# Attention scores and values as full 128-row products, lower parts of the keys kept beside zeros

## The reference, cut to what matters

```python
# first block: 8 heads, strictly causal ("mixer")
z = einsum('bhqd,bhkd->bhqk', q_blk, k_c) * scale       # 128 queries, keys 0..end
sp = where(valid, softplus(z), 0.0)
rem = cumsum(sp, axis=3, reverse=True) - sp
a = where(valid, exp(log_sigmoid(z) - rem), 0.0)
outs.append(einsum('bhqk,bhkd->bhqd', a, v_c))

# second block: 16 heads ("fox")
s = einsum('bhqd,bhkd->bhqk', q[:, :, lo:hi], k[:, :, :hi]) * scale
s = s + cum[:, :, lo:hi, None] - cum[:, :, None, :hi]
s = where(kpos[None, :] <= qpos[:, None], s, -1e30)
outs.append(einsum('bhqk,bhkd->bhqd', softmax(s), v[:, :, :hi]))
```

## Time and profile before

| | before |
|---|---|
| median of three runs | 2120.28 us |
| time of the profiled execution | 2121.13 us |
| its span in the trace | 2119.9 us |
| PE busy | 2077.3 us (98%) |
| DVE busy | 1101.9 us (52%) |
| ACT busy | 836.4 us (39%) |
| POOL busy | 289.0 us (14%) |
| share of PE in the chain that ended last | 92% |
| granted TensorE clock, mean | 0.992 |

### The profile page before, as it was taken

The page is one execution under the profiler, slowest core; times in us unless marked ns, Lnnn a source line. Parts: engine busy times, 40 slices in busy tenths (PEclk is TensorE's granted clock), DMA queues, the critical chain, the costliest instruction groups (busy, mean ns, idle before and its releaser), DMA issues.

```text
span 2119.9 us, 24127 instructions
## 1 busy us (share of the span) xinstructions
PE 2077.3 (98%) x9440; PEld 1695.1 (80%) x9440; DVE 1101.9 (52%) x1570; ACT 836.4 (39%) x1200; POOL 289.0 (14%) x215
## 2 busy tenths in 40 slices
PE   5999999999999999999999999999999999999998
PEld 4788888788877878888888877777788888888888
DVE  8655655624554654333336444443456566464666
ACT  3322222435655533222224455554333343242343
POOL 3000000001101210000000343443000022021120
PEclk8999999999999999999999999999999999999999
DMA  7665554422223533333223332332433423232232
GB/s 289 230 198 189 190 188 131 165 101 80 70 75 100 175 109 110 100 98 92 98 76 121 127 106 100 100 105 100 173 115 129 144 91 99 99 91 98 87 98 85
DMA packets 84401, 261.31 MB, mean 123 GB/s; under 512 B 9264, under 2 KB 13488, under 8 KB 84288
## 3 DMA queue, kind: packets, MB, share of 16 engines
q1 hardware_dynamic: 84288, 259.77, 37.2%
HBM read 242.92 MB, written 16.81 MB: 123 GB/s over the span
## 4 chain that ended last, share of the span: by engine, by line
PE 92%; DVE 4%; ACT 2%; issue 1%; DMA 1%; POOL 0%; SPq 0%; DVEq 0%; ACTq 0%; POOLq 0%
PE P L729 28%; PE P L731 28%; PE P L730 28%; PE P L930 2%; DVE ADA L1925 1%; PE P L1108 1%; PE P L942 1%; PE P L941 1%; PE P L1099 0%; DMA WRAW<-w_in_zv 0%; PE P L944 0%; DVE SQ L1912 0%; PE P L834 0%; PE P L1155 0%; PE P L822 0%
## 5 line engine op out<-in xcount | busy, mean ns | idle before, releaser
L729 PE MATMUL P<-UH,WH 128*128 128x512 f32 (+1 forms) x1848 | 719.4, 389 | 12.2 <-POOL UL L2729 10.7
L731 PE MATMUL P<-UH,WL 128*128 128x512 f32 (+1 forms) x1848 | 714.3, 387 | 0.0
L730 PE MATMUL P<-UL,WH 128*128 128x512 f32 (+1 forms) x1848 | 713.7, 386 | 0.0
L584 ACT ACTIVATE WH<-WRAW 128x1024 fp32r<-128x1024 f32 (+1 forms) x345 | 359.0, 1043 | 840.0 <-PE P L731 827.4
L599 DVE TENSOR_TENSOR WL<-WRAW,WH 128x1024 fp32r<-128x1024 f32 (+1 forms) x286 | 355.1, 1245 | 206.5 <-ACT WH L584 205.8
L729 PEld LDWEIGHTS P<-UH,WH 128*128 128x128 f32 x1848 | 348.1, 188 | 86.7 <-POOL UL L2729 10.0
L731 PEld LDWEIGHTS P<-UH,WL 128*128 128x128 f32 x1848 | 347.8, 188 | 71.0
L730 PEld LDWEIGHTS P<-UL,WH 128*128 128x128 f32 x1848 | 348.1, 188 | 68.5
L729 PE MATMUL P<-AH,WH 128*128 128x512 f32 x544 | 215.6, 396 | 0.0
L731 PE MATMUL P<-AH,WL 128*128 128x512 f32 x544 | 215.2, 396 | 0.0
L730 PE MATMUL P<-AL,WH 128*128 128x512 f32 x544 | 215.1, 395 | 0.0
(11 more groups left out here) (285 smaller groups left out, 2234.2 us busy)
## 6 DMA issues: line engine op xcount, KB each, us to landing
WRAW<-w_gu SPq DMA_DIRECT2D x88, 512.0 KB, 3.5
ADA<-w_ada SPq DMA_DIRECT2D x72, 512.0 KB, 4.7
WRAW<-w_down SPq DMA_DIRECT2D x48, 512.0 KB, 3.6
WRAW<-w_up SPq DMA_DIRECT2D x44, 512.0 KB, 3.5
WRAW<-w_in SPq DMA_DIRECT2D x40, 512.0 KB, 3.5
WRAW<-w_mix SPq DMA_DIRECT2D x36, 512.0 KB, 3.4
WRAW<-w_down SPq DMA_DIRECT2D x24, 384.0 KB, 3.1
WRAW<-w_out SPq DMA_DIRECT2D x16, 512.0 KB, 4.0
```

The lines of the kernel that those rows point to most:

```text
L584: s.act.activation(hi, s.mem.WRAW[:, c % 4, :self.order[c][2]], FN.Copy).then_inc(*self.rounded.inc(c))
L729: pe.matmul(out, wh, xh, start=start, stop=False, skip_group_check=True)
L730: pe.matmul(out, wh, xl, start=False, stop=False, skip_group_check=True)
L731: return pe.matmul(out, wl, xh, start=False, stop=stop, skip_group_check=True)
```

## The change

The keys' lower part gets a tile for each head of a pair, `KL0` and `KL1`, of the same shape as `K`; the rows that the head does not own hold zeros, written once per attention by POOL (`pool_zeros`). The second product of each strip then reads 128 rows. The last block is treated as the other three: two split products of 128 columns in the scores, two in the values. `T3`, `V31`, `V32`, `P3` and the ACT copies that filled them go. In fox the transposed last block lies beside block 1 in PSUM bank 6, and one ACT copy and one DVE subtraction of 512 columns take both (they were 128 and 384 columns on ACT, 384 on DVE). The mask products and the mixer's unsplit running-sum products (lines 1007, 1009) stay as they are.

```diff
+TURNED = [(2, 4, 1024, 256), (1, 6, 512, 512), (0, 5, 0, 512)]
...
-        kl = put(e + "KL", [128, 2, S], F32R)
-        t3 = [put(e + n + "3", [128, 2, 128], F32) for n in ("Q", "K")]
+        kl = [put(e + "KL0", [128, 2, S], F32R), put(e + "KL1", [128, 2, S], F32R)]
...
-def pe_products(s, out, Q, K, KL, h, a, b, keys_first):
+def pe_products(s, out, Q, K, KL, h, a, b, keys_first, start=True):
     p, e = (h // 2) % 2, h % 2
-    rows = head_rows(h)[0]
-    for i, (q, k) in enumerate([(Q[e][:, p, a], K[e][:, p, b]),
-                                (Q[e][rows, p, a], KL[rows, p, b])]):
-        x, y = (k, q) if keys_first else (q, k)
-        s.pe.matmul(out, x, y, start=i == 0, stop=False, skip_group_check=True)
+    for i, k in enumerate((K[e], KL[e])):
+        x, y = Q[e][:, p, a], k[:, p, b]
+        if keys_first:
+            x, y = y, x
+        s.pe.matmul(out, x, y, start=start and i == 0, stop=False, skip_group_check=True)
...
-    for j in range(3):
+    for j in range(4):
         of = slice(OFF[j], OFF[j] + WID[j])
         v = V[:, j, 128 * h:128 * h + 128]
         pe.matmul(ob[:, 128 * j:S], v, hi[:, of], start=j == 0, stop=False, skip_group_check=True)
-        pe.matmul(ob[:, 128 * j:S], v, lo[:, of], start=False, stop=j == 2, skip_group_check=True)
-    rows = head_rows(h)[0]
-    pe.matmul(s.P[rows, 7, 384:S], V3[:, 64 * h:64 * h + 64], own, start=False, stop=True,
-              skip_group_check=True).then_inc(*s.value.inc(name, h))
+        last = pe.matmul(ob[:, 128 * j:S], v, lo[:, of], start=False, stop=j == 3,
+                         skip_group_check=True)
+    last.then_inc(*s.value.inc(name, h))
...
-        for j in range(3):
+        for j in range(4):
             pe_products(s, Z[:, OFF[j]:OFF[j] + WID[j]], mem.Qa, mem.Ka, mem.KLa, h,
-                        slice(128 * j, S), slice(j * 128, (j + 1) * 128), True)
-        pe.matmul(Z[:, OFF[3]:OFF[3] + 128], mem.T3a[1][rows, p, :], mem.T3a[0][rows, p, :],
-                  start=False, stop=False, skip_group_check=True)
+                        slice(128 * j, S), slice(j * 128, (j + 1) * 128), True, j < 3)
...
-            if i == 0:
-                pe.matmul(z, mem.T3b[0][rows, p, :], mem.T3b[1][rows, p, :], start=False,
-                          stop=False, skip_group_check=True)
-            else:
-                if i == 1 and h:
-                    on.wait_ge(*s.pt_lo(h - 1, 2))
-                pe_products(s, z, mem.Qb, mem.Kb, mem.KLb, h, slice(i * 128, (i + 1) * 128),
-                            slice(0, 128 * (i + 1)), False)
+            if i == 1 and h:
+                on.wait_ge(*s.pt_lo(h - 1, 2))
+            pe_products(s, z, mem.Qb, mem.Kb, mem.KLb, h, slice(i * 128, (i + 1) * 128),
+                        slice(0, 128 * (i + 1)), False, i > 0)
...
-        block(h, 3, 6, 384)
-        block(h, 1, 6, 0).then_inc(*s.turned.inc(h, 1))
+        block(h, 3, 6, 0)
+        block(h, 1, 6, 128).then_inc(*s.turned.inc(h, 1))
...
-    act.activation(T3[w][:, p % 2, :], src[:, own], FN.Copy, scale=scale)
...
 def dve_pairs(s, e, w, p, Q, K, KL, src, scale):
     s.on_dve.wait_ge(*s.qk_hi(e, w, p))
+    s.on_dve.wait_ge(*s.kl_zero(e))
...
-        lo = KL[rows, p % 2, :] if w else X[other, p % 2, :]
+        lo = KL[h][rows, p % 2, :] if w else X[other, p % 2, :]
...
+def pool_zeros(s, e, KL):
+    s.pool.memset(KL[0][:, :, :].bitcast(F32), 0.0)
+    s.pool.memset(KL[1][:, :, :].bitcast(F32), 0.0).then_inc(*s.kl_zero.inc(e))
...
     pool_norm(s, "ffn1", "start")
+    on.wait_ge(*s.ple_mm(3))
+    on.wait_ge(*s.u_lo("ffn1", KD - 1))
+    pool_zeros(s, "a", mem.KLa)
...
     pool_power(s, mem.R[:, 8:12], mem.VAR[:, 4:8], "ffn2", 1)
+    on.wait_ge(*W.done(W.at["ffn2", "down", 2, KD - 1]))
+    on.wait_ge(*s.x_row(KD - 1))
+    pool_zeros(s, "b", mem.KLb)
```

More of the change, by code:

```diff
@@ L284, in __init__ @@
         self.expo = new("expo", [(h, i) for h in range(16) for i in (3, 2, 1, 0)])
-        self.pt_hi = new("pt_hi", [(h, x) for h in range(16) for x in (2, 3, 1, 0)])
+        self.pt_hi = new("pt_hi", [(h, x) for h in range(16) for x in (2, 1, 0)])
         self.zv = new("zv", [(half, tb) for half in range(2) for tb in range(4)])
@@ L361, in __init__ @@
         self.merged = new("merged", [(m,) for m in tiles])
+        self.kl_zero = new("kl_zero", [("a",), ("b",)])
         self.prob = new("prob", [(h, i) for h in range(16) for i in (3, 2, 1, 0)])
@@ L451, in mix @@
         self.V1 = put("V1", [128, 4, 1024], F32R)
-        self.V31 = put("V31", [128, 512], F32)
         self.pairs("a")
@@ L463, in pairs @@
         k = [put(e + "K0", [128, 2, S], F32R), put(e + "K1", [128, 2, S], F32R)]
-        kl = put(e + "KL", [128, 2, S], F32R)
-        t3 = [put(e + n + "3", [128, 2, 128], F32) for n in ("Q", "K")]
+        kl = [put(e + "KL0", [128, 2, S], F32R), put(e + "KL1", [128, 2, S], F32R)]
         if e == "a":
-            self.Qa, self.Ka, self.KLa, self.T3a = q, k, kl, t3
+            self.Qa, self.Ka, self.KLa = q, k, kl
         else:
-            self.Qb, self.Kb, self.KLb, self.T3b = q, k, kl, t3
+            self.Qb, self.Kb, self.KLb = q, k, kl
     def second(self):
@@ L481, in fox @@
         self.V2 = put("V2", [128, 4, 2 * D], F32R)
-        self.V32 = put("V32", [128, D], F32)
         self.pairs("b")
-        self.P3 = put("P3", [128, 128], F32)
         self.T2 = put("T2", [128, 1280], F32)
@@ L919, in pe_first, with pe_values @@
     pe_norm(s, "ffn1", 0, s.mem.AH1, s.mem.AL1)
-def pe_products(s, out, Q, K, KL, h, a, b, keys_first):
+def pe_products(s, out, Q, K, KL, h, a, b, keys_first, start=True):
     p, e = (h // 2) % 2, h % 2
-    rows = head_rows(h)[0]
-    for i, (q, k) in enumerate([(Q[e][:, p, a], K[e][:, p, b]),
-                                (Q[e][rows, p, a], KL[rows, p, b])]):
-        x, y = (k, q) if keys_first else (q, k)
-        s.pe.matmul(out, x, y, start=i == 0, stop=False, skip_group_check=True)
-def pe_values(s, V, V3, name, h, hi, lo, own, free):
+    for i, k in enumerate((K[e], KL[e])):
[3 more added lines that the diff above has]
+        s.pe.matmul(out, x, y, start=start and i == 0, stop=False, skip_group_check=True)
+def pe_values(s, V, name, h, hi, lo, free):
     pe, ob = s.pe, s.P[:, 7, :]
@@ L976, in pe_mixer @@
     for h in range(8):
-        p, rows = (h // 2) % 2, head_rows(h)[0]
         on.wait_ge(*s.qk_lo("a", 0, h // 2))
@@ L1023, in pe_mixer @@
         free.append(s.o_sum("a", h - 1) if h else s.small)
-        pe_values(s, mem.V1, mem.V31, "a", h, mem.SH, mem.SL, own, free)
+        pe_values(s, mem.V1, "a", h, mem.SH, mem.SL, free)
     assert not fillers
@@ L1125, in values @@
         free.append(s.o_sum("b", h - 1) if h else s.small)
-        pe_values(s, mem.V2, mem.V32, "b", h, mem.PH, mem.PL, mem.P3[:, :], free)
+        pe_values(s, mem.V2, "b", h, mem.PH, mem.PL, free)
     fill()
@@ L1401, in act_first_square, with act_pairs @@
     act_square(s, "ffn1", m, s.mem.H[:, m, :], s.sums("start", 0))
-def act_pairs(s, e, w, p, Q, K, T3, src, own, scale, free):
+def act_pairs(s, e, w, p, Q, K, src, scale, free):
     act, on = s.act, s.on_act
@@ L1440, in v_evac @@
         on.wait_ge(*s.u_lo("ffn1", KD - 1))
[L1441 to L1444, removed]
+        act.activation(hi, by_head(src), FN.Copy).then_inc(*s.v_hi.inc("mix v", tb))
     def ga_evac(m):
@@ L1455, in qk_evac @@
         free = [W.done(W.at[tag]), s.score("a", 2 * p - 3) if p >= 2 else s.sums("ffn1", 0)]
-        act_pairs(s, "a", w, p, mem.Qa, mem.Ka, mem.T3a, s.psum(*tag), slice(384, 512),
-                  0.125 if w == 0 else 1.0, free)
+        act_pairs(s, "a", w, p, mem.Qa, mem.Ka, s.psum(*tag), 0.125 if w == 0 else 1.0, free)
     def evac(kind, m):
@@ L1630, in v_evac @@
         on.wait_ge(*W.done(W.at["ffn2", "down", 2, KD - 1]))
[L1631 to L1634, removed]
+        act.activation(hi, by_head(src), FN.Copy, scale=r).then_inc(
+            *s.v_hi.inc("fox v", half, tb))
     def qk_evac(w, p):
         free = [s.qk_raw(w, p), s.score("b", 2 * p - 3) if p >= 2 else s.sums("ffn2", 1)]
-        act_pairs(s, "b", w, p, mem.Qb, mem.Kb, mem.T3b, mem.TMP[:, w, :], slice(0, 128), 1.0,
-                  free)
+        act_pairs(s, "b", w, p, mem.Qb, mem.Kb, mem.TMP[:, w, :], 1.0, free)
     for q in range(4):
@@ L1689, in turned @@
     def turned(h):
-        def upper(j, bank, n):
+        for j, bank, at, n in TURNED:
             on.wait_ge(*s.turned(h, j))
@@ L1693, in upper @@
                 on.wait_ge(*s.value("b", h - 1))
-            act.activation(mem.PH[:, OFF[j]:OFF[j] + n], s.P[:, bank, 0:n], FN.Copy).then_inc(
+            act.activation(mem.PH[:, at:at + n], s.P[:, bank, 0:n], FN.Copy).then_inc(
                 *s.pt_hi.inc(h, j))
[L1697 to L1703, removed]
     fill(1)
@@ L2416, in turned @@
     def turned(h):
-        for j, bank, w in ((2, 4, 256), (1, 6, 384), (0, 5, 512)):
-            x = slice(OFF[j], OFF[j] + w)
+        for j, bank, at, w in TURNED:
```

(1 more changed line is left out.)

## The result

| | before | changed |
|---|---|---|
| median | 2120.36 us (4 runs, 2119.91 to 2120.60) | 2086.74 us (4 runs, 2085.97 to 2086.94) |
| profiled execution | 2121.13 us, span 2119.9 | 2086.63 us, span 2085.4 |

The ratio is 0.984, with a 95% interval from 0.9828 to 0.9853: 33.6 us faster. The forecast was 2101.7 us with a range from 2088.0 to 2111.0. The direction was right; the gain is 1.8 times the one forecast, and the time lies just under the range.

The account below looks back on a forecast made before the run. PE, busy 98% of the span, was taken as the bound. Savings of 7.2 + 10.7 + 2.1 + 0.2 = 20.2 us less 1.6 given back, net 18.6, took 2120.28 to 2101.7 us; range 2088 to 2111.

Parts of the forecast that it names:

- mixer scores: Mixer, first score product to masks: 2.45 us becomes 1.55, saving 0.90 per head, 7.2 us in 8 heads.
- mixer values and next scores: Mixer values, 1.50 us before, save 0.02 per head, 0.2 us in all; the scores that follow save 0.90.
- fox scores: Fox's score products with four masks: 2.95 us becomes 2.28, saving 0.67 per head, 10.7 us in 16 heads.
- fox values: Fox's value products: 1.61 us becomes 1.48, saving 0.13 per head, 2.1 us in 16 heads.
- given back in the mixer: Mixer savings lost to waits: 1.4 us in heads 1 and 3, 0.1 each in heads 6 and 7; 1.6 in all.
- x: Cost of a 128-column split product, two in each head's scores and two in its values, 96 in all; taken as 0.22 us.
- The rival with x = 0.11: Narrow split products in scores and values are cheap: 28.8 us saved, 2091.5 us; chance 0.33.
- s: Passage from a full-row product into a bf16 mask, one per mixer head, four per fox head, 72 in all; taken as 0.07 us.
- The rival's other end: Cheap narrow split products at x = 0.06: 33.6 us saved, 2086.7 us; the cheap-products case had chance 0.33.
- The mechanism: In score pairs, each passage from 128 to 64 rows or back costs about 0.19 us; the change takes it out.
- The give-back at `RL`: Mixer line 1015, PE waiting for DVE's RL: heads 1 and 3 gain 0.2, not 0.90, each; 1.4 us back.
- The rival with dear masks: Masks cost more than the rows did: s = 0.33 leaves no gain, s = 0.40 gives 2125.5 us; chance 0.03.

Follow-up runs that it names:

- The probe: Changed kernel with eight added matmuls of varied width, rows and type ahead of each fox head's values, to price them; 2112.85 us, run once, only its trace used.
- the second experiment: Changed kernel with the second product of each score pair read on the head's own 64 rows again; 2112.03 us, 25.3 slower.
- The run with both holds: Changed kernel with fox's masks last, three POOL subtractions in the mixer held until RL, and the next ones in heads 1 and 3 held too; 2081.66 us.

## Why the prediction was wrong

The table sets the forecast's savings per head beside what the timelines of both kernels show. A phase is read from its first product to the second product of the filler behind it, less 0.23. It is the same within 0.03 us in every head, but for the first head of each attention.

| term | forecast saved | measured | in all |
|---|---|---|---|
| mixer scores | 0.90 | 1.19 (2.72 to 1.53, head 0) | with values |
| mixer values and next scores | 0.92 | 1.45 (4.24 to 2.79) x 7; last values 0.34 | 11.7 us, for 7.4 |
| fox scores | 0.67 | 1.20 in head 0, 1.13 in 15 | 18.2 us, for 10.7 |
| fox values | 0.13 | 0.34 x 16 | 5.4 us, for 2.1 |
| given back in the mixer | 1.6 in all | 1.1 x 2 in heads 1 and 3, 0.08 and 0.32 in 6 and 7 | 2.6 us |

11.7 + 18.2 + 5.4 - 2.6 = 32.7 us, of 34.5 between the two profiled executions. Read from their first score to their last value, the attentions are 9.15 and 23.85 us shorter, 33.0 in all. Of the other 1.5, 0.5 is a shorter wait for DVE at the program's start (6.1 for 6.6 us), which is 6.7 and 5.3 in other executions of unchanged code there. Another 1.0 is TensorE's clock behind fox, in code that the change does not touch. PE waits there for `ZV` and then runs at the lower of its two levels: the granted clock is 0.51 of full in both kernels, and products of 512 columns start 0.43 us apart, until they start 0.23 apart again. Before, from 1530.41 to 1536.05, 13 products:

```profile
1530.41 0.79 PE L729 MATMUL P<-WH,UH 128*128 128x512 f32 x1 [4.74 <-ACT ZV L1724]
...
1536.05 0.40 PE L730 MATMUL P<-WL,UH 128*128 128x512 f32 x1
```

After, from 1496.79 to 1500.31, 8 products:

```profile
1496.79 0.77 PE L731 MATMUL P<-WH,UH 128*128 128x512 f32 x1 [4.78 <-ACT ZV L1701]
...
1500.31 0.40 PE L733 MATMUL P<-WH,UL 128*128 128x512 f32 x1
```

Over full speed this stretch costs 2.7 us before and 1.7 after. In the profiled executions of the experiments it costs between 1.5 and 3.0, in the same lines of code, so it is not counted as a gain of the change. Some 0.3 us or less is left that is not traced to a row.

**The step that failed is x, the 128-column split product.** I took 0.22 us, from the unsplit rows of the same width and element size; it is 0.06 + 0.11 for a pair in the scores and 0.11 each in the values with what follows. 96 products at 0.12 less on average are 11.5 us. The error was to take width and element size for what sets the price, when the 16 unsplit records were two to a matmul, and the row of the same kind of product, 256 columns at 0.11, should have been the upper bound of any narrower one. The probe shows both: 0.105 for float32r and 0.21 for unsplit at 128 columns. The rival with x = 0.11 was named with a third of the chance; its 2091.5 is still 4.8 us too slow.

**The second is s.** The passage into the mask was put down at 0.07 by symmetry with the way back; it is 0 to 0.01. 72 passages: 5.0 us. Without it the rival gives 2086.5, and 2086.74 was measured. That number stood in the forecast, as the sum with both costs at their lower ends, and the range was stopped at 2088, short of it. The agreement to 0.2 us is partly luck: x came out a little under 0.11, the start behind fox's transposes took 0.08 more than forecast in 15 heads, the mixer gave back 2.6 and not 2.0, and what varies outside the attentions, up to 1.5 us, added to the gain. The rival's other end, x = 0.06 with s = 0.07, gives 2086.7 too; the time alone can't tell the two apart, the rows of the timeline and the probe do.

**What held.** The mechanism: passages between 128 and 64 rows cost 0.20 us each at 512 columns, 0.19 at 256 and 0.14 at 128 beyond the price of the product, and they were most of what the change took out; two experiments and the probe show it, and the second experiment alone brings back 25.2 of the 33.0 us. The Trainium skill, TensorEngine Tiling (Array Packing), "Key Properties", has the rule that a change of tiling mode drains the engine, without a number; the probe agrees with it, at 0.14 to 0.20 us a change. The give-back at `RL` was right in its place, heads 1 and 3 and not 2, 4 and 5. It came out at 1.1 us a head for 0.7: the scores saved 1.16 and not 0.90, and PE's way from the first score to the first value became only 0.05 and 0.08 us shorter in these heads, where 0.2 had been put down for the copy into `T3`. Of the 2.38 us tap in that chain I had not seen that it was a collision. Fox has no wait but one of 0.2 us; the zeros took 0.96 us a memset and nobody waited. The rival with dear masks was far off.

## What to carry to other kernels

Read a matmul's price from the distance to the next start, and split it into columns and passages: a product on fewer rows than its neighbours costs more than one padded with zeros, and the surcharge is per change, so beside the price of the product it weighs most on narrow ones. For an operation that the trace does not have, an upper bound from the same kind of operation at a larger size binds more than a likeness in shape to another kind. When PE is the bound and a stage is shortened, look where it already runs level with another engine: there the saving stops, and the next thing to shorten is that engine's longest abnormal duration.

## What the runs showed of the hardware

- A change between 128 and 64 contraction rows costs 0.20 us at 512 columns, 0.19 at 256, 0.14 at 128; a run on 64 rows pays only at its two ends (eight of 512 columns: 2.06 us, and 0.09 and 0.11 more on the products ahead and behind, against 1.83 on 128 rows).
- float32r in a run costs 0.23, 0.12, 0.11, 0.105, 0.10 us at 512, 256, 192, 128, 64 columns; behind wider products the first 128-column one took 0.06. Unsplit float32 of 128 columns costs 0.21. In turn with float32r of 512 columns a pair costs 0.43 to 0.45, no more than the two by themselves (0.44).
- A bf16 mask product behind a float32r one costs nothing extra; the float32r product behind it takes 0.07 to 0.09 us more. Whether the type is the cause is open, for behind narrow float32r products the next one takes 0.05 to 0.09 more as well.
- Behind a wait of 4.7 us PE's products of 512 columns start 0.43 us apart (granted clock 0.51), and later 0.23. Over full speed this cost between 1.5 and 3.0 us in the profiled executions.
- DVE operations with two inputs in SBUF are held up while POOL's subtraction, begun earlier, runs, and end 0.55 and 1.34 us after it, a little less than their own usual duration: 2.38 us for 0.75, 3.32 for 1.49. The Trainium skill, SBUF — State Buffer, "Who interferes with whom", says so of exactly this pair of kinds, and that POOL instructions that only write don't do it; the trace agrees with both. The run with both holds shows the first in reverse, POOL's subtraction taking 3.46 us where DVE had begun before it. For the second, DVE's subtraction with two inputs in SBUF takes its usual 1.23 us in the changed kernel although POOL's memset of the zeros has begun before it:

```profile
417.47 0.96 POOL L2728 MEMSET aKL<- 128x1024 f32 x1 [12.61 <-DVE UL L2041]
...
417.48 1.23 DVE L601 TENSOR_TENSOR WL<-WRAW,WH 128x1024 fp32r<-128x1024 f32 x1
```
